# Three of four weight sums by VectorE, one by an adding transfer: a two-block transformer kernel on one core

## The reference

```
h = rms_norm(x, g)
gu = h @ w_gate_up                                   # or h @ wg and h @ wu
f = (silu(gu[..., :D_FF]) * gu[..., D_FF:]) @ w_down
```

## Time and profile before

| what | value |
|---|---|
| median of 3 runs | 1554.11 us (1553.86 to 1554.25) |
| profiled execution, its time | 1552.32 us |
| its span, first to last instruction | 1550.5 us |
| busy: PE, DVE, ACT, POOL | 1529.4, 1310.6, 1020.1, 155.1 us |
| share of the span: PE, DVE, ACT, POOL | 99%, 85%, 66%, 10% |
| granted TensorE clock | 0.999 of full speed |
| read from memory | 293.59 MB |

### The profile page before, as it was taken

How to read it: one execution, slowest core, us unless ns; L and a number is a source line. 1 busy time by engine, 2 the same in 40 slices (tenths; PEclk the granted TensorE clock), 3 DMA queues, 4 the chain that set the end, 5 groups by cost and what they waited for, 6 DMA issues and landing times.

```text
span 1550.5 us, 20995 instructions
## 1 busy us (share of the span) xinstructions
PE 1529.4 (99%) x8060; PEld 1261.0 (81%) x8060; DVE 1310.6 (85%) x1420; ACT 1020.1 (66%) x1400; POOL 155.1 (10%) x232
## 2 busy tenths in 40 slices
PE   9999999999999999999999999999999999999998
PEld 7778888877888888888877888888888887788886
DVE  6869998787999979998758699988999766789996
ACT  7756776675667666766558477665667556666674
POOL 1001000040100010001130000001000203000000
PEclk9999999999999999999999999999999999999999
DMA  8338888523978868897740488977799652077992
GB/s 300 132 107 257 234 259 256 190 82 111 302 229 241 271 204 244 248 296 213 222 136 2 145 238 242 295 219 247 237 273 263 209 187 82 1 242 234 291 260 86
DMA packets 154611, 321.17 MB, mean 207 GB/s; under 512 B 5736, under 2 KB 50016, under 8 KB 151440
## 3 DMA queue, kind: packets, MB, share of 16 engines
q1 hardware_dynamic: 135408, 261.87, 48.5%
q0 software_dynamic: 18672, 57.42, 18.9%
q10 hardware_dynamic: 432, 0.53, 0.1%
HBM read 293.59 MB, written 1.05 MB: 190 GB/s over the span
## 4 chain that ended last, share of the span: by engine, by line
PE 93%; DVE 4%; ACT 2%; issue 1%; DMA 0%; POOL 0%; SPq 0%; POOLq 0%; DVEq 0%; ACTq 0%
PE pair L2897 10%; PE pair L2894 10%; PE pair L2893 10%; PE pair L2804 8%; PE bank L2978 6%; PE bank L2970 6%; PE bank L2974 6%; PE bank L2774 6%; PE pair L2808 4%; PE bank L2747 3%; PE bank L2680 2%; PE bank L2681 2%; PE bank L2682 2%; PE pair L3184 1%; PE pair L2953 1%; PE bank L3235 1%
## 5 line engine op out<-in xcount | busy, mean ns | idle before, releaser
L1688 DVE TENSOR_TENSOR w_lo<-raw,w_hi 128x2048 fp32r<-128x2048 f32 (+2 forms) x167 | 378.7, 2271 | 47.9 <-ACT w_hi L1052 47.5
L1052 ACT ACTIVATE w_hi<-raw 128x2048 fp32r<-128x2048 f32 (+2 forms) x171 | 324.8, 1903 | 84.8 <-PE bank L2978 26.9
L1688 DVE TENSOR_TENSOR w_lo<-fold_raw,w_hi 128x2048 fp32r<-128x2048 f32 x144 | 327.7, 2286 | 13.2 <-ACT w_hi L1052 13.1
L1052 ACT ACTIVATE w_hi<-fold_raw 128x2048 fp32r<-128x2048 f32 x144 | 275.8, 1915 | 73.6 <-PE bank L2978 44.6
L2894 PE MATMUL pair<-w_hi,xs_lo 128*128 128x512 f32 x384 | 149.9, 390 | 0.0
L2893 PE MATMUL pair<-w_hi,xs_hi 128*128 128x512 f32 x384 | 149.7, 390 | 0.0
L2804 PE MATMUL pair<-xt,w_hi 128*128 128x512 f32 x528 | 129.0, 394 | 0.1
L2893 PE MATMUL pair<-w_hi,xt 128*128 128x512 f32 x288 | 113.8, 395 | 0.0
L2804 PEld LDWEIGHTS pair<-xt,w_hi 128*128 128x128 f32 x528 | 97.3, 188 | 19.5 <-issue 0.5
L2894 PE MATMUL pair<-w_hi,xt 128*128 128x512 f32 x288 | 112.3, 390 | 0.0
L2970 PE MATMUL bank<-w_hi,hid_hi 128*128 128x512 f32 x424 | 106.3, 390 | 0.0
(11 more groups left out here) (362 smaller groups left out, 2853.8 us busy)
## 6 DMA issues: line engine op xcount, KB each, us to landing
raw<-in_ffn_wd SPq DMA_DIRECT2D x44, 1024.0 KB, 9.4
fold_raw<-in_w_gate_up SPq DMA_DIRECT2D x32, 1024.0 KB, 7.1
fold_raw<-in_ffn_wu SPq DMA_DIRECT2D x32, 1024.0 KB, 6.8
fold_raw<-in_ffn_wg SPq DMA_DIRECT2D x32, 1024.0 KB, 7.1
fold_raw<-fold_raw POOLq DMA_DIRECT2D x24, 1024.0 KB, 8.2
raw<-in_w_down SPq DMA_DIRECT2D x22, 1024.0 KB, 9.3
raw<-in_w_in SPq DMA_DIRECT2D x21, 1024.0 KB, 5.5
fold_raw<-in_ffn_wu POOLq DMA_DIRECT2D x16, 1024.0 KB, 11.8
```

The lines of the kernel that those rows point to most:

```text
L1052: act.activation(w_hi[u % RING][:, 0:filled(u)], raw_of(u)[:, 0:filled(u)], ACT.Copy)\
L1688: dve.tensor_tensor(w_lo[s][:, 0:filled(u)], raw_of(u)[:, 0:filled(u)], w_hi[s][:, 0:filled(u)].bitcast(F32), ALU.subtract)\
```

## The change

`right_sum(k)` on DVE takes the place of the adding transfer `add_right`: it adds RIGHT into UPPER. The second read of that quarter from memory goes, and POOL's list holds only `add_to_lower`. `RIGHT_SUM` now counts by 1 (`SUM_STEP`). `load_right(k)` gets one more wait, since RIGHT is read once more. The lists of SP, ACT and DVE in all six networks are rearranged. PE's list is unchanged. The diff, with parts of the lists left out:

```diff
-SUM_STEP = (1, 16, 1, 16)
+SUM_STEP = (1, 1, 1, 16)
...
                     if k:
                         sp.wait_ge(fold_made[THREE_SUM], fold_index(f, k))
+                        sp.wait_ge(fold_made[RIGHT_SUM], fold_index(f, k))
...
+                load_left(2)
                 load_upper(2)
-                load_left(2)
...
+                load_left(3)
                 load_upper(3)
-                load_left(3)
...
-            def add_right(f, k):
-
-                _, _, wu, _, _ = ffns[f]
-                pool.wait_ge(fold_landed[UPPER], 16 * (fold_index(f, k) + 1))
-                pool.wait_ge(fold_made[UPPER_SUM], fold_index(f, k) + 1)
-                pool.dma_start(quarters(UPPER), quarter(wu, 1, 256 * FOLD_GROUPS[k][0]), accum_op=ALU.add)\
-                    .then_inc(fold_made[RIGHT_SUM], 16)
...
                 for k in range(FOLDS):
-                    add_right(f, k)
                     add_to_lower(f, k)
...
+                down_rounded(0)
                 silu(0)
-                down_rounded(0)
                 hidden_rounded(0)
...
                 fifth_out(1)
+                fold_hidden(0, 1)
                 sum_rounded(1, 5)
...
+                first_out(2)
                 fold_hidden(1, 0)
-                sum_rounded(2, 2)
                 sum_rounded(2, 3)
-                first_out(2)
...
+                def right_sum(k):
+
+                    landed(k, RIGHT)
+                    dve.wait_ge(fold_made[UPPER_SUM], fold_index(f, k) + 1)
+                    dve.tensor_tensor(fold_raw[UPPER][:, :], fold_raw[UPPER][:, :], fold_raw[RIGHT][:, :], ALU.add)\
+                       .then_inc(fold_made[RIGHT_SUM], 1)
...
                 add_cross(0)
+                row_sums()
                 split_lo(u0 + GATE_AT[1])
+                add_up(0)
                 row_factors_out()
+                split_lo(u0 + UP_AT[1])
                 scale_gates(0)
-                row_sums()
-                add_up(0)
-                split_lo(u0 + UP_AT[1])
+                split_lo(u0 + DOWN_AT[0])
                 multiply(0)
-                split_lo(u0 + DOWN_AT[0])
+                upper_sum(0)
                 hidden_rest(0)
-                upper_sum(0)
+                add_cross(1)
+                row_sums_rest()
                 split_lo(u0 + GATE_AT[2])
...
                 three_sum(1)
+                split_lo(u0 + FOLD_AT[1][2])
                 fold_rest(0, 0)
-                split_lo(u0 + FOLD_AT[1][2])
                 split_lo(u0 + FOLD_AT[1][3])
+                right_sum(1)
                 split_lo(u0 + FOLD_AT[1][4])
                 split_lo(u0 + FOLD_AT[1][5])
+                first_up(1)
+                split_lo(u0 + DOWN_AT[3])
+                fold_rest(0, 1)
                 first_gate(1)
...
                 three_sum(3)
                 split_lo(u0 + FOLD_AT[3][2])
                 split_lo(u0 + FOLD_AT[3][3])
+                right_sum(3)
                 split_lo(u0 + FOLD_AT[3][4])
```

More of the change, by code:

```diff
@@ L806, in _ @@
                 load_lower(0)
+                load_down(1)
                 load_down(2)
-                load_down(1)
                 load_left(1)
@@ L1291, in fold_hidden @@
                     act.activation(hid_hi[g % 2][:, :], bank[2 + b], ACT.Copy).then_inc(hidden_hi, 1)
+                gate_cross_out(0)
                 gate_rounded(1)
-                gate_cross_out(0)
+                up_cross_out(0)
                 up_rounded(1)
-                up_cross_out(0)
+                down_rounded(0)
                 silu(0)
-                down_rounded(0)
                 hidden_rounded(0)
+                gate_cross_out(1)
                 row_sums_rounded()
+                up_cross_out(1)
                 gate_rounded(2)
-                up_cross_out(1)
-                gate_cross_out(1)
                 up_rounded(2)
-                silu(1)
                 quarter_rounded(0, 0)
                 gate_cross_out(2)
+                silu(1)
                 quarter_rounded(0, 1)
+                hidden_rounded(1)
+                up_cross_out(2)
+                sum_rounded(0, 2)
+                sum_rounded(0, 3)
                 silu(2)
-                hidden_rounded(1)
-                sum_rounded(0, 2)
-                up_cross_out(2)
                 first_out(0)
-                sum_rounded(0, 3)
                 quarter_rounded(0, 4)
-                hidden_rounded(2)
                 fifth_out(0)
@@ L1320, in ffn @@
                 down_rounded(1)
+                hidden_rounded(2)
                 fold_act(0, 0)
@@ L1338, in ffn @@
                 down_rounded(4)
-                fold_hidden(0, 1)
+                third_out(1)
                 fold_act(1, 0)
-                third_out(1)
                 quarter_rounded(2, 0)
@@ L1363, in ffn @@
                 sum_rounded(3, 2)
-                fold_hidden(2, 1)
+                first_out(3)
                 sum_rounded(3, 3)
-                first_out(3)
                 quarter_rounded(3, 4)
                 fifth_out(3)
+                fold_hidden(2, 1)
                 sum_rounded(3, 5)
@@ L1920, in ffn @@
                 add_cross(0)
+                row_sums()
                 split_lo(u0 + GATE_AT[1])
+                add_up(0)
                 row_factors_out()
+                split_lo(u0 + UP_AT[1])
                 scale_gates(0)
-                row_sums()
-                add_up(0)
-                split_lo(u0 + UP_AT[1])
+                split_lo(u0 + DOWN_AT[0])
                 multiply(0)
-                split_lo(u0 + DOWN_AT[0])
+                upper_sum(0)
                 hidden_rest(0)
-                upper_sum(0)
+                add_cross(1)
+                row_sums_rest()
                 split_lo(u0 + GATE_AT[2])
-                add_cross(1)
+                add_up(1)
+                split_lo(u0 + UP_AT[2])
                 scale_gates(1)
-                split_lo(u0 + UP_AT[2])
-                add_up(1)
                 split_lo(u0 + FOLD_AT[0][0])
+                three_sum(0)
                 multiply(1)
-                three_sum(0)
                 add_cross(2)
+                split_lo(u0 + FOLD_AT[0][1])
+                right_sum(0)
+                add_up(2)
                 scale_gates(2)
-                split_lo(u0 + FOLD_AT[0][1])
-                row_sums_rest()
                 split_lo(u0 + FOLD_AT[0][2])
-                add_up(2)
+                multiply(2)
                 split_lo(u0 + FOLD_AT[0][3])
-                multiply(2)
                 split_lo(u0 + FOLD_AT[0][4])
-                first_gate(0)
                 hidden_rest(1)
                 split_lo(u0 + FOLD_AT[0][5])
+                first_gate(0)
+                split_lo(u0 + DOWN_AT[1])
                 first_up(0)
-                split_lo(u0 + DOWN_AT[1])
                 split_lo(u0 + FOLD_AT[0][6])
                 hidden_rest(2)
-                second_up(0)
                 split_lo(u0 + DOWN_AT[2])
                 upper_sum(1)
+                fold_multiply(0, 0)
+                second_up(0)
                 second_gate(0)
-                fold_multiply(0, 0)
                 split_lo(u0 + FOLD_AT[1][0])
@@ L1977, in ffn @@
                 second_gate(1)
-                second_up(1)
+                split_lo(u0 + FOLD_AT[2][0])
                 fold_multiply(1, 1)
-                split_lo(u0 + FOLD_AT[2][0])
                 split_lo(u0 + FOLD_AT[2][1])
-                fold_rest(1, 0)
                 three_sum(2)
                 split_lo(u0 + FOLD_AT[2][2])
+                fold_rest(1, 0)
                 split_lo(u0 + FOLD_AT[2][3])
+                right_sum(2)
                 split_lo(u0 + FOLD_AT[2][4])
+                first_gate(2)
                 split_lo(u0 + FOLD_AT[2][5])
                 fold_rest(1, 1)
-                first_gate(2)
                 split_lo(u0 + DOWN_AT[5])
+                second_up(2)
                 split_lo(u0 + FOLD_AT[2][6])
-                second_up(2)
                 first_up(2)
                 split_lo(u0 + DOWN_AT[6])
-                fold_multiply(2, 0)
                 upper_sum(3)
                 second_gate(2)
+                fold_multiply(2, 0)
                 split_lo(u0 + FOLD_AT[3][0])
@@ L2012, in ffn @@
                 split_lo(u0 + DOWN_AT[8])
-                fold_multiply(3, 0)
                 second_gate(3)
```

18 lines of the change are left out of this document (9 added, 9 removed).

## The result

The changed kernel takes 1564.37 us (median of 4 runs, 1563.88 to 1565.5) against 1553.98 for the kernel before. The ratio is 1.0072, 95% interval 1.006 to 1.0084. By the medians it is slower by 10.4 us, where I had forecast 8.5.

A forecast was written before the change was run, and what follows sets the result against it. PE was taken to bound the kernel, busy 99% of the span. The waits at the first down product (5.4 us) and in the sets (3.1) summed to 8.5 us over a median of 1554.1: forecast 1562.5 us, range 1555.5 to 1570.5.

The forecast's parts named there:

- PE-bound, nothing to win: Between first gate and last down unit PE has no time to win; removing 24 MB of transfers gains 0.
- The wait at the first down product, 5.4 us: down(0) waits for hidden_rest(0), now behind upper_sum(0): 1.42 us in networks 0 to 2, 1.0 in 4; bounds 0 to 13.
- The waits in the sets, 3.1 us: DVE late for PE in sets 1 to 3: 0.35 us in networks 0, 1, 0.6 in 2 to 5; bounds 0 to 9.
- DVE's need of 31.2 us a set: DVE's work per set with the added sum, 0.2 us short of PE in networks 0, 1, 0.36 in 2 to 5.
- The estimate of 33.0 us by the Trainium skill's rule: DVE's need per set if each operation waits for an empty pipe, 2 us more than PE; the prediction went by the trace.
- Edits at nothing: LEFT loaded ahead of UPPER, load_right(k)'s extra wait and POOL's remaining transfer cost 0; without cover, perhaps 1 us a set.
- Covered: Rival: the lateness at down(0) is hidden and the sets fit; 1554 to 1557 us, chance 0.14.
- faster: Rival: less traffic gives PE a better cadence or earlier loads, 11 us gained, 1543 us; chance 0.05.
- standing backlog: Rival: handshake gaps bring DVE to 31.7 us a set, 18 sets cost 14 us beyond the 5.4, 1573 us; chance 0.15.

The follow-up runs named there:

- a_rest_first: Changed kernel with hidden_rest(0) put back ahead of upper_sum(0) on DVE, nothing else; ratio 1.0068 to the kernel before.
- a_sets_rests: Changed kernel with fold_rest(0, 0) and fold_rest(1, 0) moved ahead in DVE's list, upper_sum(0) still ahead of hidden_rest(0); ratio 1.006 to the kernel before.
- a_best: Changed kernel with hidden_rest(0), fold_rest(0, 0), fold_rest(1, 0) moved ahead, DVE's head reordered, ACT's head as in the kernel before; 1557.97 us, ratio 1.0031.
- a_double: Changed kernel with three_sum made twice, 24 more DVE steps of 2.2 us; ratio 1.0456 to the kernel before.
- b_sum_alone: Kernel before with right_sum(k) on DVE behind the split of place 3 replacing the adding transfer, lists otherwise in old order; ratio 1.01.

## Why the prediction was right, and where it was not

**PE-bound, nothing to win.** Right. The window without waits (network 0, set 3) is 28.28 us long before and after, with 25.2 MB less traffic. No run was faster than the kernel before.

**The wait at the first down product, 5.4 us.** The place, the releaser and the pattern over the networks were right: 1.60, 1.67, 1.63, 0.18, 1.21, 0.19 measured against 1.42, 1.42, 1.40, 0, 1.0, 0 and 0.05 for a handshake in four of them. The term was mis-sized by 1.1 us in all, as a wait costs 0.14 us from record to record and another 0.1 us or so in the product behind it.

**What that term meant.** Here the prediction's reading was incomplete. It put the 5.4 us down to the position of one call, and `a_rest_first` shows that moving that call gives back only 1.3 us. Both are true: the call alone costs 10.5 us on the old kernel, where DVE has room later on, but with the sums added DVE is late at set 1 in any case. The step that I left out is the walk of DVE's queue from the first down product to set 1, which holds one sum more than before. I started at set 1 with the times of the kernel before, as if DVE were on time there. It is on time only because PE has been made 1.6 us late at the down product. With PE on time, in `a_rest_first`, networks 0, 1, 2 and 4 lose 0.2 to 0.5 us in set 0 and 1.0 to 1.2 in set 1. So the two terms are not independent as my sum has them, and that the sum came near is partly luck.

**The waits in the sets, 3.1 us.** 4.1 measured, and one of the two places was wrong. `fold_rest(0, 0)` was forecast 0.15 us late and is 0.19, plus 0.11 in the next product. From there on I had the whole lateness come out at the third product of set 3. In fact the fifth product of set 2 takes it first (0.19 to 0.39 us), as `fold_rest(1, 0)` has the least slack there, and set 3 loses only 0.3 us in all. My own numbers for this place were also not consistent: 0.35 us in network 0 and 0.34 more in networks 2 to 5 make 0.69 each and 3.5 us in all, where I wrote 0.6 and 3.1. `a_sets_rests` moves it to the place that I had named.

**DVE's need of 31.2 us a set.** Right, and the most useful number. In `a_best` DVE's round measures 31.22 us and set 3 loses about what is over PE's, and in `a_double` about 50 of 55 us beyond it are exposed. The estimate of 33.0 us by the Trainium skill's rule (VectorE: DVE Perf Modes, "The DRAIN you can't avoid") does not hold here: set 2 of the changed kernel takes 31.22 us with that work in it. The same section also says that an operation which is not held starts earlier, which the prediction left out; the starts 2.20 us apart beside records of 2.28 agree with that.

**Edits at nothing.** The loads' order cost nothing. The removed transfers gained nothing.

**The rivals.** Covered and faster did not come. The standing backlog (14 us in the sets) did not either. `b_sum_alone` comes near its size, 13.6 us in the old order, but 5.6 of these are the late `multiply(2)` in set 0, and 8.0 lie in sets 1 to 3.

## What to carry to other kernels

Before moving work onto an engine that feeds the bottleneck, add up what that engine needs per round from start-to-start times and compare it with the bottleneck's round: here 31.2 against 31.0 us, where 24 steps of 2.20 us cost 3.7 us in the best order found and 10.6 in the changed kernel's. With 24 more, at 33.4 us, another 60.8 came on top. A wait that shows up in the profile is where the lateness comes out, not always what makes it: take it away and see whether the time comes back or the next wait grows. With a list of instructions that is the same in two kernels, match the k-th instruction of both; it shows losses of 0.1 us that the table of waits leaves out. Look at the granted clock of a run before pricing its work: a long wait can slow what comes after it.

## What the hardware showed beyond that

**A wait of TensorE costs a little extra behind it.** After a fifth product that had to wait, the next product starts later than usual (changed kernel, then the kernel before's 187.90 to 188.13 us, 0.23):

```profile
189.61 0.50 PE L2896 MATMUL pair<-w_hi,xs_hi 128*128 128x512 f32 x1
189.94 0.40 PE L2897 MATMUL pair<-w_hi,xs_lo 128*128 128x512 f32 x1
```

0.33 us in place of 0.23. It is 0.10 to 0.12 us at each of the 12 such waits of the changed kernel, so a lateness of 0.19 us costs 0.30. At the first down product it is 0.07. The weight loads (PEld) show where it comes from (changed kernel, then kernel before, the load for the same fifth product):

```profile
189.60 0.19 PEld L2896 LDWEIGHTS pair<-w_hi,xs_hi 128*128 128x128 f32 x1 [0.45 <-DVE hid_lo L1914]
...
187.68 0.19 PEld L2893 LDWEIGHTS pair<-w_hi,xs_hi 128*128 128x128 f32 x1
```

In the kernel before the load starts 0.22 us ahead of its product (187.90), while the product in front still runs. In the changed kernel it starts 0.01 us ahead of it, so the wait holds the load too. The product's record is then 0.50 us long in place of 0.39. No run isolates this further.

**Long waits brought a slower clock in some cases.** In `a_double` TensorE stood still twelve times for 2.2 to 3.2 us. At seven of these waits the granted clock is 0.50 (1.2 GHz) for 3.4 or 6.8 us, beginning during the wait or up to 0.9 us after its end; at the other five, of the same lengths, it stays at 1.00. In the changed kernel, where no wait in the networks is over 1.44 us, it stays at 1.00 up to the last product.

**The opening differs between executions.** In the first 10 us PE's start moves by up to 1.7 us from one execution to another with the same code there (the changed kernel -0.1, `a_rest_first` +1.6), all at a granted clock of 1.00. A difference of one profiled run below 2 us says nothing before this is taken out.
